# Expert steps in fours on 32x32 tiles of the array

## The reference

```python
def block(xb):                                   # xb: normed tokens
    qry = (xb @ w_query).reshape(T, 8, 2, 128)
    sc = einsum('thpd,pnd->thpn', qry, sub_keys)  # 128 keys, two halves
    s1, i1 = top_k(sc[:, :, 0], 16); s2, i2 = top_k(sc[:, :, 1], 16)
    # 256 candidate sums, the best 16 kept: idx (T, 8, 16), top_s
    gate = softmax(top_s)
    act = gelu(einsum('thed,td->the', u_emb[idx], xb))
    return einsum('the,thed->td', gate * act, v_emb[idx])
```

## Time and profile before

| | |
|---|---|
| median of three runs | 2196.42 us (2194.12 to 2197.8) |
| the profiled execution, span from its first to its last instruction | 2197.3 us |
| PE busy | 1761.6 us (80%), 6456 matmuls |
| DVE busy | 1405.6 us (64%) |
| POOL busy | 691.1 us (31%) |
| ACT busy | 379.4 us (17%) |
| gathers | 82944 packets, 604.02 MB, 68.9% of the DMA engines' span |
| weights, caches and other loads by SyncE | 24960 packets, 89.98 MB, 10.9% |

### The profile page before, as it was taken

The page is one execution under the profiler, slowest core; times in us unless marked ns, Lnnn a source line. Parts: engine busy times, 40 slices in busy tenths (PEclk is TensorE's granted clock), DMA queues, the critical chain, the costliest instruction groups (busy, mean ns, idle before and its releaser), DMA issues.

```text
span 2197.3 us, 21194 instructions
## 1 busy us (share of the span) xinstructions
PE 1761.6 (80%) x6456; PEld 1001.9 (46%) x6456; DVE 1405.6 (64%) x3449; ACT 379.4 (17%) x1208; POOL 691.1 (31%) x738
## 2 busy tenths in 40 slices
PE   7978888777767778988698875998878877777776
PEld 6767875323223325754265542554445543322222
DVE  4464258877777774356446887554665896766665
ACT  2242022100000002142202111101421101111111
POOL 2032101334434451233223221333333324444441
PEclk9989999898878889999799987999889988999999
DMA  4310226889998999999688975999989978999997
GB/s 148 116 75 1 68 87 249 324 330 388 388 388 354 383 383 376 372 327 359 264 319 339 390 299 197 398 418 421 363 318 419 408 293 331 390 422 422 422 422 303
DMA packets 108846, 696.16 MB, mean 317 GB/s; under 512 B 12640, under 2 KB 12768, under 8 KB 34528
## 3 DMA queue, kind: packets, MB, share of 16 engines
q0 software_dynamic: 82944, 604.02, 68.9%
q1 hardware_dynamic: 24960, 89.98, 10.9%
q10 hardware_dynamic: 864, 1.16, 0.1%
HBM read 690.20 MB, written 4.90 MB: 316 GB/s over the span
## 4 chain that ended last, share of the span: by engine, by line
PE 45%; DVE 23%; DMA 19%; issue 7%; ACT 3%; POOL 1%; DVEq 0%; POOLq 0%; SPq 0%; ACTq 0%
PE PS L1510 21%; DMA sb_AR<-in_uv,sb_idst 19%; PE PS L1315 11%; DVE sb_AR L1131 5%; PE PS L1493 4%; DVE sb_DG L1134 2%; PE PS L1428 2%; PE PS L1591 2%; DVE sb_AR L1082 1%; DVE sb_AR L1075 1%; POOL sb_AR L510 1%; ACT sb_gl L706 1%; DVE sb_AR L1076 1%; DVE sb_AR L1079 1%; DVE sb_AR L1072 1%
## 5 line engine op out<-in xcount | busy, mean ns | idle before, releaser
L1510 PE MATMUL PS<-sb_AR,sb_DG 128*128 128x512 f32 x2304 | 1144.1, 641 | 301.1 <-DVE sb_DG L1134 285.3
L510 POOL DMA_INDIRECT sb_AR<-in_uv,sb_idst x576 | 610.8, 1060 | 1176.5 <-PE PS L1510 1118.0
L1510 PEld LDWEIGHTS PS<-sb_AR,sb_DG 128*128 128x128 f32 x2304 | 443.5, 204 | 916.7 <-DVE sb_DG L1134 463.2
L1131 DVE CUSTOM_DVE_ANT_0 sb_AR<-sb_AR,sb_Hn 128x1024 f32<-128x1024 f32 x576 | 704.6, 1223 | 160.3 <-DMA sb_AR<-in_uv,sb_idst 156.6
L1134 DVE TENSOR_SCALAR sb_DG<-sb_ident,sb_gl,sb_gst 128x128 f32<-128x128 f32 x576 | 222.7, 387 | 273.7 <-ACT sb_gl L706 273.7
L706 ACT ACTIVATE sb_gl<-sb_dots 128x1 f32<-128x1 f32 x576 | 116.7, 203 | 1228.3 <-DVE sb_dots L1131 1227.8
L1315 PE MATMUL PS<-sb_hT,sb_W 128*128 128x288 f32 (+2 forms) x1664 | 297.7, 335 | 0.8 <-ACT sb_hT L568 0.8
L1315 PEld LDWEIGHTS PS<-sb_hT,sb_W 128*128 128x128 f32 x1664 | 257.2, 192 | 64.3 <-issue 30.3
L1493 PEld LDWEIGHTS PS<-sb_W,sb_mixT 128*128 128x128 f32 x768 | 90.7, 196 | 9.8 <-issue 7.7
L1493 PE MATMUL PS<-sb_W,sb_mixT 128*128 128x128 f32 x768 | 90.9, 279 | 1.7 <-DVE sb_mixT L1045 1.7
L503 POOL COPY sb_idst<-sb_idx 128x8 uint32 (+1 forms) x72 | 24.4, 339 | 118.7 <-DVE sb_idx L1102 118.3
(11 more groups left out here) (315 smaller groups left out, 1101.6 us busy)
## 6 DMA issues: line engine op xcount, KB each, us to landing
sb_W<-in_w SPq DMA_DIRECT2D x144, 512.0 KB, 7.2
sb_AR<-in_uv,sb_idst POOLq DMA_INDIRECT x576, 11.3
sb_gB<-in_gains SPq DMA_DIRECT2D x7, 512.0 KB, 8.0
sb_AR<-in_kc SPq DMA_DIRECT2D x2, 1024.0 KB, 9.7
sb_AR<-in_vc SPq DMA_DIRECT2D x2, 1024.0 KB, 17.9
sb_X<-in_x SPq DMA_DIRECT2D x3, 512.0 KB, 5.2
out_o_v<-sb_AR SPq DMA_DIRECT2D x1, 1536.0 KB, 17.4
out_o_y<-sb_Hn SPq DMA_DIRECT2D x3, 512.0 KB, 7.4
```

The lines of the kernel that those rows point to most:

```text
L510: g.indirect_dma_start(UV[:, s, :], None, T[f"uv{l}"], bass.IndirectOffsetOnAxis(ap=idst[:, 8 * half + s:8 * half + s + 1], axis=0)).then_ ...
L1131: v.tensor_tensor_reduce(UV[:, sl, 0:D], UV[:, sl, 0:D], Hn[:, xt, :], 1.0, 0.0, ALU.mult, ALU.add, dots[:, sl:sl + 1]).then_inc(S("dots"), 1)
L1510: r = mm(PS[:, 6 + half, :], DG[:, sl, :], UV[:, sl, o:o + 512], start=False, stop=False, skip_group_check=True)
```

## The change

The unit of work is a step of four slots instead of one slot: `UNITS`, `AHEAD`, the planner's results and the loops are divided by four (`AHEAD` is 74 steps, still 296 slots), `PE_LAG` is one step. The loops still cover 16 slots per iteration.

- **VectorE** does the four dots of a step one after the other, each after the wait for its own buffer, then waits for gelu once, multiplies gelu and gate for the four slots (128x4), waits for that, and writes four diagonals in one product: `RP[:, 0:32]`, a column of four 32x32 identities, times the four weights. `DG` is 128 x 8 x 32 instead of 128 x 8 x 128. The 16-wide copy of the gates goes.
- **ScalarE** takes gelu of 128x4 once per step.
- **TensorE** waits for the diagonals once per step, on a product of zeros with one column (128 rows, 32 columns of weights). Then, for each slot and each half of 512 columns, four products of 32 rows and 32 columns of weights: row group p of `DG` and v goes to PSUM partitions p in the first half, and to partitions p + 32 (modulo 128) in the second.
- **End of a unit.** Since the second half is turned by 32 partitions, every unit's sum is now copied to `YS`, and TensorE writes it back through the identity, for the second half through a cyclic shift of it (`ident2`, the identity with its first 32 columns repeated). The sample units use `RP` as before. `YS` has memory of its own.

The diff, cut to its core:

```diff
-UNITS = ((256, 2, 0, 32), (0, 0, 32, 128), (128, 1, 160, 128), (256, 2, 288, 32), (0, 0, 320, 128), (128, 1, 448, 128))
-ACC = (2, 3, 4, 6, 7, 8)
-AHEAD = 296
-PE_LAG = 2
+UNITS = ((256, 2, 0, 8), (0, 0, 8, 32), (128, 1, 40, 32), (256, 2, 72, 8), (0, 0, 80, 32), (128, 1, 112, 32))
+AHEAD = 74
+PE_LAG = 1
...
-                plan[ps, kind, j] = int(m)
+                plan[ps, kind, j] = int(m) // 4
...
+            eng.wait_ge(S("ident"), 1)
+            ch.add(g.tensor_copy(ident2[:, 128:160], ident2[:, 0:32]))
...   # ScalarE
                 eng.wait_ge(S("dots"), at(i, m + 1))
-                o = m % UVS
-                s.activation(gl[:, o:o + 1], dots[:, o:o + 1], ACT.Gelu_apprx_tanh).then_inc(S("gelu"), 1)
+                o = 4 * (m % 2)
+                s.activation(gl[:, o:o + 4], dots[:, o:o + 4], ACT.Gelu_apprx_tanh).then_inc(S("gelu"), 1)
...   # VectorE, step
-                c, sl = m % 16, m % UVS
-                if c == 0:
-                    g0 = c0 + m - m0
-                    v.tensor_copy(gst[:, :], gate[:, g0:g0 + 16] if i is None else gate[:, bass.ds(i * 16 + g0, 16)])\
-                        .then_inc(S("gates"), 1)
-                    eng.wait_ge(S("gates"), m // 16 + 1 if i is None else i + (m // 16 + 1))
-                landed = 16 * (m // UVS + 1)
-                eng.wait_ge(S(f"uv_in{sl}"), landed if i is None else i * 32 + landed)
-                v.tensor_tensor_reduce(UV[:, sl, 0:D], UV[:, sl, 0:D], Hn[:, xt, :], 1.0, 0.0,
-                                       ALU.mult, ALU.add, dots[:, sl:sl + 1]).then_inc(S("dots"), 1)
+                landed = 16 * (m // 2 + 1)
+                for c in range(4):
+                    sl = 4 * (m % 2) + c
+                    eng.wait_ge(S(f"uv_in{sl}"), landed if i is None else i * 32 + landed)
+                    r = v.tensor_tensor_reduce(UV[:, sl, 0:D], UV[:, sl, 0:D], Hn[:, xt, :], 1.0, 0.0,
+                                               ALU.mult, ALU.add, dots[:, sl:sl + 1])
+                r.then_inc(S("dots"), 1)
+                o, g0 = 4 * (m % 2), c0 + 4 * (m - m0)
+                gt = gate[:, g0:g0 + 4] if i is None else gate[:, bass.ds(i * 16 + g0, 4)]
                 eng.wait_ge(S("gelu"), at(i, m + 1))
-                v.tensor_scalar(DG[:, sl, :], ident[:, :], gl[:, sl:sl + 1], gst[:, c:c + 1],
-                                ALU.mult, ALU.mult).then_inc(S("diag"), 1)
-                if c == 15:
-                    eng.wait_ge(S("diag"), at(i, m + 1))
+                v.tensor_tensor(gst[:, o:o + 4], gl[:, o:o + 4], gt, ALU.mult).then_inc(S("gates"), 1)
+                eng.wait_ge(S("gates"), at(i, m + 1))
+                v.tensor_tensor(DG[:, o:o + 4, :], RP[:, 0:32].unsqueeze(1).to_broadcast([128, 4, 32]),
+                                gst[:, o:o + 4].unsqueeze(2).to_broadcast([128, 4, 32]), ALU.mult).then_inc(S("diag"), 1)
...   # VectorE, end of a unit: for every unit, not for the sample alone
+                eng.wait_ge(S("acc"), 2 * q + 1)
+                for half in range(2):
+                    v.tensor_copy(YS[:, 512 * half:512 * half + 512], PS[:, 6 + half, :]).then_inc(S("ys"), 1)
+                eng.wait_ge(S("acc"), 2 * q + 2)
...   # TensorE, step
-                sl = m % UVS
                 eng.wait_ge(S("diag"), at(i, m + 1))
-                for half in range(2):
-                    o = D + 512 * half
-                    r = mm(PS[:, 6 + half, :], DG[:, sl, :], UV[:, sl, o:o + 512], start=False, stop=False,
-                           skip_group_check=True)
-                r.then_inc(S(f"uv_free{sl}"), 1)
+                mm(PS[0:32, 6, 0:1], ZR[:, 0:32], ZR[:, 0:1], start=False, stop=False, skip_group_check=True)
+                for c in range(4):
+                    sl = 4 * (m % 2) + c
+                    for half in range(2):
+                        o = D + 512 * half
+                        for p in range(0, 128, 32):
+                            to = (p + 32 * half) % 128
+                            k = mm(PS[to:to + 32, 6 + half, :], DG[p:p + 32, sl, :], UV[p:p + 32, sl, o:o + 512],
+                                   start=False, stop=False, skip_group_check=True)
+                    k.then_inc(S(f"uv_free{sl}"), 1)
...   # TensorE, end of a unit
+                for half in range(2):
+                    eng.wait_ge(S("ys"), 2 * q + half + 1)
+                    if UNITS[q][1] == 2:
+                        k = mm(PS[:, 6 + half, :], RP[:, :], YS[:, 512 * half:512 * half + 512], start=True, stop=True)
+                    else:
+                        k = mm(PS[:, 6 + half, :], ident2[:, 32 * half:32 * half + 128],
+                               YS[:, 512 * half:512 * half + 512], start=True, stop=True)
+                k.then_inc(S("acc"), 1)
```

More of the change, by code:

```diff
@@ L58, in step_plan @@
     plan = {}
-    for ps, m, misc, qkv, head, smp, out, q in ((0, 160) + PACE[0], (1, AHEAD) + PACE[1]):
+    for ps, m, misc, qkv, head, smp, out, q in ((0, 160) + PACE[0], (1, 4 * AHEAD) + PACE[1]):
         for kind, n, k in (("norm2", 1, misc), ("qkv", 24, qkv), ("head", 10, head), ("smp", 4 * (1 - ps), smp),
@@ L285, in at @@
         def at(i, value):
-            return value if i is None else i * 16 + value
+            return value if i is None else i * 4 + value
         class Steps:
@@ L315, in loop @@
                         first(i)
-                    for c in range(16):
+                    for c in range(4):
                         self.step(m0 + c, i)
-                self.m += 16 * n
+                self.m += 4 * n
                 self.edge("end")
@@ L738, in _ @@
             gate_exp(0)
-            run.upto(16)
+            run.upto(4)
             gate_exp(1)
-            run.upto(32)
-            run.loop(32, 8)
+            run.upto(8)
+            run.loop(8, 8)
             gate_exp(2)
@@ L827, in _ @@
             mixer1(1)
-            run.upto(448)
+            run.upto(112)
             gate_exp(5)
             norm(6)
-            run.loop(448, 8)
+            run.loop(112, 8)
             norm(7)
@@ L1200, in pick_tile1 @@
                 ch.loop_end()
-            picks(0, lambda kind, j: run.upto({16: 8, 17: 16}.get(j, 0)))
+            picks(0, lambda kind, j: run.upto({16: 2, 17: 4}.get(j, 0)))
             gate_of(1)
-            run.upto(32)
-            run.loop(32, 8, pick_tile1)
+            run.upto(8)
+            run.loop(8, 8, pick_tile1)
             gate_of(2)
```

31 lines of the change are left out of this document (11 added, 20 removed).

## The result

The changed kernel takes **2224.01 us** (median of four, 2219.85 to 2227.67) against 2197.11 for the kernel before beside it (2194.12 to 2199.18): ratio 1.0115, 95% interval 1.0095 to 1.0136. It is slower, by 1.2%. I had forecast 2155 with a range of 2100 to 2222.

A forecast was written before the change was run, and what follows sets the result against it. DMA was taken to bound the last loop, with PE, DVE and pauses after picks limiting stages between 354 and 1870. Gains of 72 less losses of 29 gave -43 from 2197.3: 2155 us, range 2100 to 2222.

The forecast's parts named there:

- PE's part: TensorE sums: all eight tiles run at once, 0.86 us a slot; a step of four 3.9 us against 6.9.
- halves in turn: Rival on TensorE: the two halves run one after another, 1.72 us a slot, 7.4 a step; 2214 us total, chance 0.21.
- One bank in turn: Rival on TensorE: tiles sharing a bank exclude each other, 3.4 us a slot, 14.3 a step; 2,750 us total, chance 0.06.
- DVE's part: VectorE's dots, gate product and diagonals: four slots take 5.7 us against 7.04, saving 0.34 a slot.
- Step (1) of what is worse: Last loop: buffers held until the fourth slot lands; refill takes 5.7 to 7.2 us, under 9.9, so zero cost.
- My own list of what would be wrong: Signs against the forecast: last-loop DMA share under 0.98, PE steps over 6.9 at full clock, or clock 0.50 where 0.97.
- The first loop: Tile-1 loop, 480 to 833: eight iterations each gain 0.7 us despite a later first release after the pick, -5.
- Unit ends (2): At each prompt unit's end, copying banks and adding the turned half back costs 2.8 us more, four times, 11 us.
- term (4): Stage borders: the group waits for its fourth slot, eight times 2 us, 16 us in all; bounds 0 to 60.
- The last group (3): The kernel's last group: TensorE takes 3.9 us in place of 1.72, a loss of 2.2.
- The gains: Savings summed over the stages from 354 to 1870, 72 us in all, against losses of 29.
- hidden: Rival: relief falls where DMA is full and coarser release holds buffers; gains halve, losses stay; 2190 us, chance 0.13.

The follow-up runs named there:

- e11: The changed kernel with five useless products of zeros behind each step of four in the last loop alone; 2216.18 us, ratio 1.0085.
- e5: The changed kernel with the second half on the first half's four tiles, without the copy and two products at four unit ends; 2302.13 us, ratio 1.0478.
- e1: The kernel before with the 32x32 tiles and turned second half, still one slot a step; 2159.17 us, ratio 0.9824.
- e2: The changed kernel with whole 128x128 diagonals and no turned half, so steps of four without tiles; 2313.15 us, ratio 1.0517.
- the pairs: The changed kernel with tiles kept but steps of two slots, four steps in the ring; 2147.48 us, ratio 0.9777.

## Why the prediction was wrong

**PE's part: right.** All eight tiles run at once: 64 matmuls in 3.66 us at full clock (forecast 4 x 0.86 = 3.44 behind 0.5 for the small matmul and the tilings; in e11 the whole step takes 3.8). The two rivals on the array fall; that the measured 2224 lies near the 2214 of "halves in turn" is a coincidence, since a step never took 7.4 us at full clock. "Halves in turn" is what e5 builds, 7.07 us. "One bank in turn" would be 13.8; the Trainium skill's rule in "TensorEngine Tiling (Array Packing)", "Restrictions and Gotchas", that different row tiles can't access one bank at the same time, doesn't show in this trace: each half's four tiles have four row groups and one bank, and they overlap. The turn's own cost is the unit ends.

**DVE's part: right.** Dots 1.14 apart when their data is there, gelu 0.38 to wait, gate 0.16, diagonals 0.29: some 5.5 us per four against 5.7 forecast.

**Step (1) of what is worse, "the DMA stays full, zero cost": this is the step that failed.** I set 5.7 to 7.2 us against a cover of 9.9 (my terms give 7.0 for the upper end, not 7.2). The chain measures 9.7. What I left out, in its order:

```
                                            forecast           measured (2030.12 to 2039.86)
last byte to the dot's start                    -                  1.34
dot, gelu, gate, diagonals to PE               2.0                 2.16
PE to the first release (half clock)         1.7 to 3.0            2.28
release to first byte                      2, issue in it          3.96 = 0.74 + 1.84 issue + 1.38
```

What went wrong is the time from the last byte to the start of the dot, which I had not listed (1.34), and the way from the release to the first byte, which I had guessed as 2 and which is 4.0, with an issue of 1.84 where the earlier trace rows show 0.96. The cover of 9.9 was right to 0.3. I had called 2.7 us a margin, and 3.3 us of the chain were missing from it, less 0.7 that I had too much in PE's part. The half clock I had in the range, as a step of no consequence: e11 prices it at the whole loss of the last loop from slot 464 on. It is worth 0.85 us on PE and, through the dot that the issue then meets, about 0.9 on POOL, together more than the margin of some 1.6 that the estimate above gives at full clock. My own list of what would be wrong had "a DMA share in the last loop under 0.98" and "a clock of 0.50 where it was 0.97"; 0.98 and 0.73 are what came.

**The first loop, forecast -5, came to some +14** (1.76 us in each of eight iterations; +24.4 with the border behind it). The two first releases were forecast at 8.1 and "near 6.5" us after the pick; they measure 8.60 and 6.49. So the working had the answer, 1.6 x 8 = +13, and I argued it away with the group before the pick being freed late. The table of eight kernels shows that nothing offsets it.

**Unit ends (2), 2.8 us each: right in size, wrong in number.** At the end of the kernel the copy starts at 2206.00 and the residual at 2208.76, so 2.76 against the 2.77 of the earlier trace rows, and e1, which has the turned end but single slots, has a tail 2.6 us longer than before. At the first border, slots 144 to 160, e1 loses nothing at all: other work covers it. The fours lose 12 there with tiles and 13 without (e2), where the pairs lose 4.2 and 2.9. So the borders' price is the grouping's, more than the 2 us each of my term (4), inside its bounds of 0 to 60. The last group (3) was forecast at 2.2; with PE at half clock its sum takes 5.2 us with the small matmul, where the last slot took 1.98 before: 3.2.

**The gains.** 833 to 950: -20.7, forecast -9, but it begins with what the border had just lost. 1094 to 1158: -5.0, forecast -6. 950 to 1094: -5.2 of -13; 1158 to 1350: +0.3 of -13; 1555 to 1650: -1.1 of -6; 1730 to 1870: +1.0 of -11. In 1158 to 1350 the pairs show that the gain exists (-10.4), and that the fours spend it; in 1730 to 1870 they have -2.6. That a group holds the ring there too until its fourth slot is in, as the "hidden" rival said, is my reading; no run changes these stages alone. The sum, from the table's column and 1.1 us at its start: gains 1.1 + 20.7 + 5.2 + 5.0 + 0.7 = 32.7, losses 4.1 + 24.4 + 0.3 + 4.0 + 14.2 + 6.4 = 53.4, so +20.7 of the +20.8 on the profiled execution's span (2197.3 to 2218.1).

**What stays open.** The split of the twelve us at the borders between the group's late fourth slot and PE's lag of a whole step was not tried by itself. Nor were more buffers, which by the margin should free the fours, nor the half clock without the longer issue.

## What to carry to other kernels

When work is grouped over a ring, write the whole loop from last byte to next first byte as a list, with the time from last byte to the waiting instruction, the issuing engine and its queue in it, and set it against what the other groups cover, (ring - group) x one transfer; here a saving on two engines was worth less than nothing once the difference went to zero. A quicker engine may be a slower one: PE with longer pauses ran at 0.73 of its clock where it had 0.99, and its time to the first result is what the ring sees. A delay can also move one engine's work onto another's: look at what each start of the chain meets. Split the two parts of a change before judging it: here the tiles gain 41 to 89 us at every group size, the grouping of four costs 65 even with them, and pairs with single releases behind the picks turn +27 us into -66.

## What the runs showed of the hardware

- Eight 32x32 tiles in eight different places of the array, two banks, run at once, float32: 64 matmuls of 512 columns in 3.66 us at full clock, 5.3 to 6.5 in most steps of the changed kernel's last loop, where the clock is at half for a part or all of them. On four places the same 64 take 7.07 at full clock.
- An indirect DMA's issue on POOL that begins while DVE's dot runs ends 0.89 us (0.88 to 0.91, 10th to 90th percentile of 140) after that dot's end, as if it had started only then; else it takes 0.94 in the median (436 issues). The same in the kernel before (121 and 455). An issue that begins before the dot isn't held. The longest took 2.0 us in place of 0.94, the one in the cycle shown 1.84, and the releases' timing decides who meets it.
- TensorE's granted clock may be 0.66 over a whole loop (e1) at no cost, and useless products that hold it at 1.00 can make a loop faster (e11).
- From a gather's last byte to the start of the dot that waits for it: 1.1 to 1.4 us (e11, where every cycle is alike), 1.34 in the cycle shown.
- One product of 128x512 with two broadcast operands took DVE 692 ns, of 128x128 292, of 128x64 225.
